# Expert blocks of 32 token slots on quarters of TensorE instead of 64 on halves

## The chip, the cores and the metric

The kernel runs on one core of a Trainium2 chip. The metric is the device time of one execution in microseconds. Its median before the change is 1385.75 us over three runs (1383.36 to 1388.35). All data are float32.

## The reference

A backbone of two layers over 512 latent tokens of width 1024 (with 256 context tokens for the attention of layer 0). Layer 0 mixes tokens by attention, layer 1 by a chunked gMLP; after each comes a mixture of 16 experts with hidden width 512, of which every token takes two. The change lies in the mixture. Cut to what matters:

```python
def moe_ffn(t, w_router, router_bias, w_gate, w_up, w_down):
    scores = jax.nn.sigmoid((t @ w_router).astype(jnp.float32))
    sel = scores + router_bias.astype(jnp.float32)
    ...                                  # best group of 4 experts, then the best 2 in it: eidx
    wts = jnp.take_along_axis(scores, eidx, 1)
    wts = wts / jnp.sum(wts, -1, keepdims=True)
    ...                                  # assignments sorted by expert, padded to blocks
    def expert_block(args):
        xblk, e = args
        hid = jax.nn.silu(xblk @ w_gate[e]) * (xblk @ w_up[e])
        return hid @ w_down[e]
    yb = lax.map(expert_block, (xb, block_e)).reshape(n_rows, d)
    y = jnp.zeros((n_tok + 1, d), jnp.float32).at[row_tok].add(yb.astype(jnp.float32) * row_w[:, None])
    return y[:n_tok].astype(t.dtype)
```

## The kernel before, in words

`backbone` writes one program for each engine; semaphores order them. SP issues all loads of weights, ACT (ScalarE) the stores, POOL (GpSimd) the gathers.

**Routing.** In `moe(l)` VectorE chooses two experts for each token, TensorE ranks the assignments by a product with a triangle, and VectorE computes how many blocks of BLK = 64 slots each expert needs (at least one), the table of the experts' first blocks, and each assignment's slot. Which token sits in a slot is found block by block: `onehot` compares the slots with 0 to 63 for both assignments (L956 to L958) and steps the slots back by 64 (L959), `index` on TensorE multiplies the one-hot with the token numbers (L1264), and VectorE casts the column to int32 as `gidx` (L962). Three such rounds come before the first block, and one lies in each block. 

**Gathers.** An indirect DMA (L437) fetches the 64 token rows of a block into `xga`. A GpSimd copy (L442) hands them to `xg`, and the next gather starts then: one is in flight.

**A block.** The loop runs over the blocks of an expert. TensorE waits for the turned rows `xT` and the expert's gate and up weights, then for each half h of the hidden width multiplies 64 slots by 256 columns of gate (L1301, PSUM partitions 0 to 63) and of up (L1303, partitions 64 to 127), side by side on two halves of its columns. After each half ScalarE takes silu of the gate part (L641), and VectorE multiplies by the up part (L995), while TensorE goes on with the other half. TensorE turns the hidden rows (L1311), ScalarE copies them out of PSUM (L643), and the down product (L1327) runs in two groups of eight records, 512 columns each, the index product between them. In the same block the next block's rows are turned (L1269) and VectorE applies scale and shift (L965, L967). VectorE multiplies the output by the gate row (L1005), and ScalarE issues two stores to `expert_rows` (L648). A matmul of float32 shows as two records.

The loops of ScalarE, VectorE and GpSimd take two blocks in each turn; where the number of blocks is odd, TensorE hands them an empty one at the end. ScalarE's loop begins with a small Silu (L636), before which its activation table is loaded.

**Weights.** Gate, up and down of an expert are 2 MB each. There are three sets of buffers. `follow` on SP waits until an expert's last block is through gate and up (for down: through the down product), and then issues the loads of the expert three further on into the same buffers (L302). At each change of expert TensorE reads that expert's first and last block from the table (L1284, L1285).

At the end of the mixture GpSimd waits for the stores and gathers for each token its two rows (L472), and VectorE adds them to the tokens.

## Time and profile before

| what | value |
|---|---|
| median of 3 runs | 1385.75 us |
| the profiled execution | 1385.64 us, span 1383.9 us |
| PE busy | 1173.4 us (85%) |
| PE weight loads busy | 662.0 us (48%) |
| DVE busy | 543.8 us (39%) |
| ACT busy | 245.3 us (18%) |
| POOL busy | 191.8 us (14%) |
| moved by DMA | 335.32 MB, mean 242 GB/s |
| granted TensorE clock, mean | 0.924 of full speed |

PE is TensorE's matmuls, PEld its weight loads, which overlap them, DVE is VectorE. The span runs from the first to the last instruction; the execution's own time is 1.7 us longer. Waits and the issue of DMAs are not counted as busy; rows with ACTq or SPq are such issues. The granted clock is told as a share of full speed: 1.00 is 2.4 GHz and 0.50 is 1.2 GHz.

### The profile page before, as it was taken

The page shows a single profiled execution, that of the slowest core. Times are in us where ns is not written, and L with a number is a line of the kernel's source. Part 1 is how long each engine was busy: PE and PEld are TensorE (multiplying, and loading weights), DVE is VectorE, ACT ScalarE, POOL GpSimd, SP SyncE. Part 2 cuts the span into 40 slices and gives each one's busy share as a digit, 9 for nine tenths or more (in the row PEclk, how much of TensorE's full clock was granted, in tenths as well). Part 3 has the DMA queues.
Part 4 walks back from the last instruction along what each step waited for, and adds up shares of the span by engine and source line. Part 5 has one row for each costly group of instructions (what it writes and reads, how often), then busy time and mean ns, then how long its engine had stood idle before and what let it go on. Part 6 is the DMA issues. An engine that isn't in the chain of part 4 may idle for free.

```text
span 1383.9 us, 18949 instructions
## 1 busy us (share of the span) xinstructions
PE 1173.4 (85%) x6946; PEld 662.0 (48%) x6947; DVE 543.8 (39%) x1319; ACT 245.3 (18%) x606; POOL 191.8 (14%) x166
## 2 busy tenths in 40 slices
PE   3999799998985999999983399999679999999940
PEld 0444344454453665665542244444445666655620
DVE  0246543462465333333323603045543333333338
ACT  0212333342020111111112111010201111111110
POOL 0012000000001111111111332200011111111123
PEclk9999999998985999999987699999679999999975
DMA  9921499980045999739995681121659996689933
GB/s 328 382 73 61 144 357 347 363 308 31 31 169 190 359 383 377 260 106 365 380 379 200 234 298 61 61 91 47 257 193 380 379 375 212 227 284 374 371 122 129
DMA packets 142758, 335.32 MB, mean 242 GB/s; under 512 B 6872, under 2 KB 9344, under 8 KB 142592
## 3 DMA queue, kind: packets, MB, share of 16 engines
q1 hardware_dynamic: 122400, 286.88, 57.0%
q10 hardware_dynamic: 13696, 25.38, 5.5%
q0 software_dynamic: 6624, 22.55, 5.4%
q8 instruction: 24, 0.39, 0.1%
q14 instruction: 14, 0.11, 0.0%
HBM read 315.40 MB, written 27.79 MB: 248 GB/s over the span
## 4 chain that ended last, share of the span: by engine, by line
PE 74%; DVE 9%; DMA 6%; SPq 6%; issue 2%; ACT 1%; POOL 0%; ACTq 0%; DVEq 0%; PEldq 0%; POOLq 0%
PE PS L1301 13%; PE PS L1327 11%; PE PS L1303 9%; PE PS L1234 8%; PE PS L1385 8%; PE PS L1144 7%; SPq L302 4%; PE PS L1164 3%; PE PS L1080 3%; PE PS L1264 2%; PE PS L1175 2%; DMA ring<-in_e_up_dram 2%; DMA RD<-expert_rows,yidx 2%; PE PS L1311 2%; PE PS L1269 2%
## 5 line engine op out<-in xcount | busy, mean ns | idle before, releaser
L1301 PE MATMUL PS<-ring,RE 128*64 128x256 f32 x1120 | 254.9, 387 | 22.4 <-DVE RE L967 10.3
L1303 PE MATMUL PS<-ring,RE 128*64 128x256 f32 x1120 | 255.3, 387 | 0.0
L1301 PEld LDWEIGHTS PS<-ring,RE 128*64 128x64 f32 x1120 | 154.6, 140 | 80.2 <-issue 45.3
L995 DVE TENSOR_TENSOR RE<-RE,PS 64x256 f32<-64x256 f32 x100 | 42.3, 423 | 350.0 <-ACT RE L641 350.0
L1303 PEld LDWEIGHTS PS<-ring,RE 128*64 128x64 f32 x1120 | 154.7, 140 | 28.6 <-issue 7.0
L1327 PE MATMUL PS<-ring,RE 128*64 128x512 f32 x560 | 136.2, 602 | 0.0
L1234 PE MATMUL PS<-ring,uT 128*128 128x512 f32 x256 | 111.2, 593 | 1.9 <-ACT G L605 1.1
L1385 PE MATMUL PS<-ring,uT 128*128 128x512 f32 x256 | 110.0, 592 | 0.0
L442 POOL COPY RFW<-RE 64x1024 f32<-64x1024 f32 x50 | 51.5, 1031 | 409.4 <-PE PS L1269 380.1
L1301 PE MATMUL PS<-uT,RE 128*64 128x256 f32 x416 | 95.0, 388 | 4.9 <-DMA RD<-in_e_up_dram 3.9
L1303 PE MATMUL PS<-RD,RE 128*64 128x256 f32 x416 | 95.3, 388 | 0.0
L1144 PE MATMUL PS<-ring,uT 128*128 128x512 f32 x192 | 84.4, 592 | 0.0
L1385 PEld LDWEIGHTS PS<-ring,uT 128*128 128x128 f32 x256 | 48.6, 190 | 60.7 <-issue 60.7
L1234 PEld LDWEIGHTS PS<-ring,uT 128*128 128x128 f32 x256 | 48.2, 190 | 60.7 <-issue 58.4
L437 POOL DMA_INDIRECT RE<-tokens,gidx x52 | 58.3, 1121 | 123.4 <-DVE gidx L962 121.9
L643 ACT ACTIVATE RE<-PS 128x128 f32<-128x128 f32 x100 | 27.7, 277 | 260.9 <-PE PS L1311 258.2
L641 ACT ACTIVATE RE<-PS 64x256 f32<-64x256 f32 x100 | 36.9, 369 | 202.0 <-PE PS L1303 193.1
L1301 PEld LDWEIGHTS PS<-uT,RE 128*64 128x64 f32 x416 | 57.5, 140 | 28.3 <-issue 15.5
L1080 PE MATMUL PS<-ring,silu_c 128*32 128x512 f32 x384 | 51.3, 655 | 23.2 <-DMA ring<-in_w_ada_dram 15.4
L1303 PEld LDWEIGHTS PS<-RD,RE 128*64 128x64 f32 x416 | 57.4, 140 | 6.6 <-issue 1.6
L437 POOL DMA_INDIRECT RFW<-tokens,gidx x2 | 2.3, 1166 | 398.0 <-DVE gidx L962 398.0
L1327 PEld LDWEIGHTS PS<-ring,RE 128*64 128x64 f32 x560 | 38.5, 136 | 39.4 <-issue 37.0
(214 smaller groups left out, 1482.3 us busy)
## 6 DMA issues: line engine op xcount, KB each, us to landing
ring<-in_w_ada_dram SPq DMA_DIRECT2D x24, 2048.0 KB, 11.7
ring<-in_e_gate_dram SPq DMA_DIRECT2D x22, 2048.0 KB, 16.6
ring<-in_e_up_dram SPq DMA_DIRECT2D x22, 2048.0 KB, 19.3
ring<-in_e_down_dram SPq DMA_DIRECT2D x22, 2048.0 KB, 19.9
uT<-in_e_gate_dram SPq DMA_DIRECT2D x10, 2048.0 KB, 17.0
RD<-in_e_up_dram SPq DMA_DIRECT2D x10, 2048.0 KB
RFW<-in_e_down_dram SPq DMA_DIRECT2D x10, 2048.0 KB, 21.9
ring<-in_b_win_dram SPq DMA_DIRECT2D x4, 2048.0 KB, 8.2
```

Source lines behind the costliest of these rows:

```text
L302: sp.dma_start(dst, src).then_inc(w_in[b], 16)
L437: nc.gpsimd.indirect_dma_start(out=rows, out_offset=None, in_=hscr[l], in_offset=bass.IndirectOffsetOnAxis(ap=gidx[0:BLK, par:par + 1], ax ...
L442: nc.gpsimd.tensor_copy(xg, xga).then_inc(xg_rd[l], 1)
L995: V_.tensor_tensor(hid[:, 256 * h:256 * h + 256], gs[:, 256 * h:256 * h + 256], PS[BLK:P, h, 0:256], ALU.mult).then_inc(hid_rd[l][h], 1)
L1080: ins = mm(PS[32 * g:32 * g + 32, bank, :], silu_c[:, k, :], w[:, k, :], start=(kk == 0), stop=(kk == 1))
L1144: ins = mm(PS[:, 4 + i % 3, :], a[:, k, j * P:(j + 1) * P], w[:, k, :], start=(k == 0), stop=(k == DC - 1))
L1164: ins = mm(PS[:, 6, :], V[:, k, kv * HD:(kv + 1) * HD], PT[:, k, :], start=(k == 0), stop=(k == NKT - 1))
L1234: ins = mm(PS[:, 2 * (j % 2) + half, :], uT[:, k, j * P:(j + 1) * P], w[half][:, k, :], start=(k == 0), stop=(k == DC - 1))
L1301: mm(PS[0:BLK, h, 0:256], xT[:, k, :], wg[:, k, 256 * h:256 * h + 256], start=(k == 0), stop=(k == DC - 1))
L1303: ins = mm(PS[BLK:P, h, 0:256], xT[:, k, :], wu[:, k, 256 * h:256 * h + 256], start=(k == 0), stop=(k == DC - 1))
L1327: ins = mm(PS[BLK * half:BLK * half + BLK, 5, :], hidT[:, k, :], wd[:, k, 512 * half:512 * half + 512], start=(k == 0), stop=(k == FC - 1))
L1385: ins = mm(PS[:, 4 + i % 4, :], uT[:, k, j * P:(j + 1) * P], w[:, k, :], start=(k == 0), stop=(k == DC - 1))
```

## The change

BLK becomes 32. The four parts of gate and up (gate and up, each in two halves of 256 columns) become four matmuls side by side on 32 columns each of TensorE, in one PSUM bank; one semaphore releases all of them. The gate parts lie on partitions 0 to 63 and the up parts on 64 to 127, so silu and product now take 64 partitions of 128 columns, twice. The hidden rows are turned in two turnings of 64 partitions, and the down product runs on four quarters of 256 columns each, so that a block leaves in four stores of 32 rows and 256 columns. The token numbers of all blocks (NCOL = 52 columns at most, with four spare) come from one accumulated product before the loop: a slot is cut into its low five bits and the rest, each is made one-hot, the second scaled by the token number. Gathers go to two buffers in turn, each by a column that GpSimd first copies to `gcol`; `xg` is now on RE. The number of blocks that the tables allow for grows from 32 to 48, and the compare with the thresholds from 7 to 15 for each expert.

```diff
-BLK = 64
+BLK = 32
+CG = P // BLK
...
                 pool.wait_ge(ix_rd[l], 1)
-                gather(0, xg, x0_in[l])
-                pool.wait_ge(ix_rd[l], 2)
-                gather(1)
+                gather(xg, x0_in[l], gidx[:, 0:1])
+                gather(xga[1], xg_in[l][1], gidx[:, 1:2])
+                gather(xga[0], xg_in[l][0], gidx[:, 2:3])
...
                         g = gg * 2 + par
-                        pool.wait_ge(xg_in[l], g * 16 + 16)
+                        pool.wait_ge(xg_in[l][1 - par], gg * 16 + 16)
+                        pool.nop(nofuse=True)
+                        nc.gpsimd.tensor_copy(gcol[:, 1 - par:2 - par], gidx[:, bass.ds(g + 3, 1)]).then_inc(gc_used[l], 1)
                         pool.wait_ge(xt_pe[l], g + 1)
                         pool.nop(nofuse=True)
-                        hand_over()
-                        pool.wait_ge(ix_rd[l], g + 3)
+                        nc.gpsimd.tensor_copy(xg, xga[1 - par]).then_inc(xg_rd[l], 1)
+                        pool.wait_ge(gc_used[l], g + 1)
...
-                        gather(par)
+                        gather(xga[1 - par], xg_in[l][1 - par], gcol[:, 1 - par:2 - par])
...
                 with act.Fori(0, pairs) as gg:
                     A(warm[:, :], ones[:, 0:1], ACT.Silu)
                     for par in range(2):
                         g = gg * 2 + par
+                        act.wait_ge(gu[l], g + 1)
                         for h in range(2):
-                            act.wait_ge(gu[l][h], g + 1)
-                            A(gs[:, 256 * h:256 * h + 256], PS[0:BLK, h, 0:256], ACT.Silu).then_inc(silu_rd[l][h], 1)
+                            A(gs[:, P * h:P * h + P], PS[0:2 * BLK, 0, P * h:P * h + P], ACT.Silu).then_inc(silu_rd[l][h], 1)
+                        for h in range(2):
                             act.wait_ge(ht_pe[l][h], g + 1)
-                            A(hidT[:, 2 * h:2 * h + 2, :], PS[:, 3 + h, 0:2 * BLK].rearrange("p (k s) -> p k s", k=2),
+                            A(hidT[:, h, :, :], PS[:, 3 + h, 0:2 * BLK].rearrange("p (h s) -> p h s", h=2),
                               ACT.Copy).then_inc(ht_rd[l][h], 1)
                         act.wait_ge(y_ev[l], g + 1)
                         act.nop(nofuse=True)
-                        for q in range(2):
-                            act.dma_start(yscr[l][bass.ds(g * BLK, BLK), 512 * q:512 * q + 512],
+                        for q in range(CG):
+                            act.dma_start(yscr[l][bass.ds(g * BLK, BLK), 256 * q:256 * q + 256],
                                           ysb[par][BLK * q:BLK * q + BLK, :]).then_inc(y_st[l][par], 16)
...
+                link(V_.tensor_copy(yidx[:, :, :], slot[:, :, :]))
+                link(V_.tensor_scalar(sli[:, :, :], yidx[:, :, :], BLK - 1, None, ALU.bitwise_and))
+                link(V_.tensor_copy(slo[:, :, :], sli[:, :, :]))
+                link(V_.tensor_tensor(shi[:, :, :], slot[:, :, :], slo[:, :, :], ALU.subtract))
+                V_.tensor_tensor(ohlo, slo[:, :, :].rearrange("p k t -> p (k t)").unsqueeze(2).broadcast_to([P, 2 * NT, BLK]),
+                                 iota_s.unsqueeze(1).broadcast_to([P, 2 * NT, BLK]), ALU.is_equal)
+                for k in range(2):
+                    for j in range(NT):
+                        ins = V_.tensor_scalar(ohhi[:, NT * k + j, :], iota_b, shi[:, k, j:j + 1], tokid[:, j:j + 1],
+                                               ALU.is_equal, ALU.mult)
+                ins.then_inc(oh_rd[l], 1)
+                dve.wait_ge(ix_pe[l], 1)
+                V_.tensor_copy(gidx[:, :], PS[0:BLK, 6, 0:NCOL]).then_inc(ix_rd[l], 1)
...
-                onehot(link)
-                for b in range(3):
-                    if b == 2:
-                        dve.wait_ge(x0_in[l], 16)
-                    dve.wait_ge(ix_pe[l], b + 1)
-                    index(b % 2)
-                    onehot(link)
                 affine(l, NT - 2)
...
                         dve.wait_ge(xt_pe[l], g + 2)
                         x_evac(lnk)
-                        dve.wait_ge(xg_in[l], g * 16 + 16)
-                        dve.wait_ge(ix_pe[l], g + 4)
-                        index(1 - par)
-                        onehot(lnk)
...
+                pe.wait_ge(oh_rd[l], 1)
+                for n in range(2 * NT):
+                    ins = mm(PS[0:BLK, 6, 0:NCOL], ohlo[:, n, :], ohhi[:, n, :], start=(n == 0), stop=(n == 2 * NT - 1))
+                ins.then_inc(ix_pe[l], 1)
...
-                        for h in range(2):
-                            for k in range(DC):
-                                mm(PS[0:BLK, h, 0:256], xT[:, k, :], wg[:, k, 256 * h:256 * h + 256],
-                                   start=(k == 0), stop=(k == DC - 1))
-                                ins = mm(PS[BLK:P, h, 0:256], xT[:, k, :], wu[:, k, 256 * h:256 * h + 256],
+                        for k in range(DC):
+                            for q in range(CG):
+                                w, h = (wg, wu)[q // 2], q % 2
+                                ins = mm(PS[BLK * q:BLK * q + BLK, 0, 0:256], xT[:, k, :], w[:, k, 256 * h:256 * h + 256],
                                          start=(k == 0), stop=(k == DC - 1))
-                            ins.then_inc(gu[l][h], 1)
...
-                        turn_hidden(0)
+                        ins.then_inc(gu[l], 1)
                         pe.wait_ge(xg_rd[l], g + 1)
                         pe.nop(nofuse=True)
                         turn_x()
+                        for h in range(2):
+                            pe.wait_ge(hid_rd[l][h], g + 1)
+                            pe.nop(nofuse=True)
+                            nc.tensor.transpose(PS[:, 3 + h, 0:2 * BLK], hid[:, P * h:P * h + P],
+                                                ident[0:2 * BLK, 0:2 * BLK]).then_inc(ht_pe[l][h], 1)
                         landed(2)
...
+                            for k in (h, h + 2):
+                                for q in range(CG):
+                                    ins = mm(PS[BLK * q:BLK * q + BLK, 5, 0:256], hidT[:, h, k // 2, :],
+                                             wd[:, k, 256 * q:256 * q + 256], start=(k == 0), stop=(k == FC - 1))
+                        ins.then_inc(dn_pe[l], 1)
```

## Rows read from the trace of the kernel before

**Rows 1.** Windows over the two expert loops: busy (records) by engine, granted clock, DMA share, GB/s.
```profile
437.50:741.10 303.60, 290.56 (x2300) 177.36 (x2300) 99.22 (x231) 43.01 (x114) 48.74 (x46) 0.97 0.87 308
1016.20:1329.50 313.30, 309.34 (x2500) 190.42 (x2500) 107.56 (x251) 46.66 (x124) 53.12 (x50) 0.99 0.85 302
```

**Rows 2.** Timeline of PE, layer 0, expert 7 and its end: start us, us, engine, what.
```profile
589.88 0.38 PE L1303 MATMUL PS<-ring,RE 128*64 128x256 f32 x1
...
596.60 0.38 PE L1301 MATMUL PS<-ring,RE 128*64 128x256 f32 x1
596.91 0.33 PE L1311 MATMUL PS<-ident,RE 64*128 64x64 f32 x2
597.08 0.67 PE L1269 MATMUL PS<-ident,RFW 64*128 64x64 f32 x8
597.70 1.94 PE L1327 MATMUL PS<-ring,RE 128*64 128x512 f32 x8
...
600.27 1.95 PE L1327 MATMUL PS<-ring,RE 128*64 128x512 f32 x8
602.04 0.38 PE L1303 MATMUL PS<-ring,RE 128*64 128x256 f32 x1
...
624.60 1.95 PE L1327 MATMUL PS<-ring,RE 128*64 128x512 f32 x8
626.65 0.40 PE L1301 MATMUL PS<-uT,RE 128*64 128x256 f32 x1
```

**Rows 3.** Window in the tail of layer 0's expert loop, columns as in rows 1.
```profile
640.00:730.00 90.00, 79.58 (x611) 47.53 (x609) 25.47 (x60) 12.93 (x32) 12.86 (x12) 0.94 1.04 379
```

**Rows 4.** Groups by line, whole span: busy us, mean ns of one, idle before and releaser.
```profile
L636 ACT ACT_TABLE_LOAD x25 | 32.1, 1283 | 119.4 <-issue 104.0 <-DVE table L941 15.4
```

**Rows 5.** Timeline of PE in the attention of layer 0.
```profile
161.04 1.92 PE L1080 MATMUL PS<-ring,silu_c 128*32 128x512 f32 x16
```

**Rows 6.** Timeline of ACT beside the block of rows 2.
```profile
591.13 1.14 ACTq L648 DMA_DIRECT2D expert_rows<-RFW  x2
592.58 1.28 ACT L636 ACT_TABLE_LOAD   x1 [4.52 <-issue]
...
593.98 0.36 ACT L641 ACTIVATE RE<-PS 64x256 f32<-64x256 f32 x1
597.28 0.28 ACT L643 ACTIVATE RE<-PS 128x128 f32<-128x128 f32 x1 [2.94 <-PE PS L1311]
```

**Rows 7.** Timeline of DVE beside the same block.
```profile
590.22 0.69 DVE L1005 TENSOR_TENSOR RFW<-PS,G 128x512 f32<-128x512 f32 x1 [0.53 <-PE PS L1327]
594.38 0.42 DVE L995 TENSOR_TENSOR RE<-RE,PS 64x256 f32<-64x256 f32 x1 [3.46 <-ACT RE L641]
```

**Rows 8.** Timeline at the start of layer 0's expert loop, POOL and PE.
```profile
433.69 1.18 POOL L442 COPY RFW<-RE 64x1024 f32<-64x1024 f32 x1 [6.61 <-DMA RE<-tokens,gidx]
...
437.54 0.68 PE L1301 MATMUL PS<-ring,RE 128*64 128x256 f32 x1 [5.09 <-DVE RE L967]
```

**Rows 9.** Timeline after the last matmul of layer 0's expert loop, DVE and POOL.
```profile
741.38 0.69 DVE L1005 TENSOR_TENSOR RE<-PS,G 128x512 f32<-128x512 f32 x1 [0.50 <-PE PS L1327]
...
748.34 0.69 DVE L1005 TENSOR_TENSOR RFW<-PS,G 128x512 f32<-128x512 f32 x1
...
753.05 0.95 POOL L472 DMA_INDIRECT RD<-expert_rows,yidx  x1 [11.44 <-DMA expert_rows<-RFW]
```

**Rows 10.** Windows around falls of the granted clock and where it held, columns as in rows 1.
```profile
317.30:320.80 3.50, 1.69 (x12) 1.08 (x11) 2.79 (x6) 1.37 (x3) 0.00 (x0) 0.99 0.00 0
...
689.90:692.80 2.90, 0.08 (x2) 0.00 (x0) 0.69 (x1) 0.32 (x1) 0.42 (x1) 1.00 1.06 400
692.80:696.20 3.40, 3.33 (x16) 2.18 (x18) 0.00 (x0) 1.17 (x2) 0.00 (x0) 0.50 1.02 331
...
709.90:716.70 6.80, 5.92 (x28) 3.75 (x30) 0.00 (x0) 0.00 (x0) 0.00 (x0) 0.50 1.03 360
726.00:728.90 2.90, 0.09 (x4) 0.06 (x2) 0.69 (x1) 0.34 (x1) 0.41 (x1) 1.00 1.05 398
```

More of the change, by code:

```diff
@@ L366, in follow @@
                     for j in range(3):
[L367 removed]
+                        sp.wait_ge(dn_pe[l] if j == 2 else gu[l], last)
                         sp.nop(nofuse=True)
@@ L405, in _ @@
             iota("thr", BLK, BLK, 0)
-            iota("pair", 2, 0, 0).then_inc(s_ic, 1)
+            iota("pair", 2, 0, 0)
+            iota("block", BLK, 0, 0).then_inc(s_ic, 1)
             pool.wait_ge(s_rope, 32)
```

128 lines of the change are left out of this document (45 added, 83 removed).

## The prediction, made before the change was run

> **What bounds the kernel now.** I first read the windows over the two expert loops. They last 303.6 and 313.3 us, 617 of 1383.9, and TensorE is busy for 96 and 99% of them at a granted clock of 0.97 and 0.99, while DMA moves 300 GB/s [rows 1]. TensorE's timeline says what a block is: one block starts at 589.88, the next at 602.04, so 12.16 us, or about 12.46 where the next block is another expert's. Inside are 32 steps of 0.217 us for gate and up (589.88 to 596.60, two column halves side by side), the turning, eight steps of 0.43 us for down in two groups and the index product [rows 2]. TensorE is the bound, but DMA is near: in the tail of the first layer it runs full, 379 GB/s [rows 3].
>
> **How many blocks.** ScalarE loads its table once for each pair of blocks, 25 times in all [rows 4], so 50 blocks, of which each layer's last may be padding. Counting the reference's routing for its inputs gives, over experts 0 to 15, blocks of 64 of 1 1 1 2 2 1 3 4 1 1 1 1 1 1 1 1 (23) and 1 1 1 1 1 3 2 4 2 2 1 1 1 2 1 1 (25), which agrees: 48 and two of padding. With 32 slots these become 2 1 2 3 4 2 5 8 2 2 1 2 1 2 1 1 (39) and 1 2 1 1 1 5 4 8 4 3 2 1 1 3 1 2 (40): 79 blocks, each to be under 617/79 = 7.8 us if the loops are to gain.
>
> **A block of 32, TensorE.** Do four quarters run side by side? The 16 matmuls of L1080, four quarters wide and 512 columns, take 1.92 us, which is four steps of 0.43 and a drain [rows 5]; the halves of now have the same step. So gate and up need 16 steps of 0.217: 3.47 us, and down eight of 0.217: 1.73 us. 5.2 us of matmul a block, 411 in all, against 48 x 10.4 = 499.
> But one counter now releases all of gate and up, so that silu, product, turning and copy stand open between them and down. From the block's start: the last step starts at 3.27 and ends 0.38 later, 3.65; ScalarE answers in 0.04 (596.91 + 0.33 to 597.28) [rows 2, 6]; silu of 128 columns 0.28 (the copy of 128 columns in [rows 6]), 3.97; VectorE answers in 0.04, and its product of 128 columns takes 0.29 (0.42 for 256 and 0.69 for 512 [rows 7]), 4.30; TensorE answers in 0.14 and turns in 0.28, 4.72; copy 0.04 + 0.28, TensorE 0.14: down starts at 5.18. The eight turnings of x (0.67 us [rows 2]) fit inside, the second half of the chain runs 0.2 behind the first and is hidden by down's first group. Down to next gate is 1.77 as now (600.27 to 602.04): **6.95 us**. Bounds: silu and product as dear as for 256 columns, +0.2; no turnaround between engines longer than counted, -0.1.
> The Trainium skill, TensorEngine Tiling (Array Packing), section PSUM Bottleneck, warns that packing quickens the matmuls and not the reading of PSUM; by matmul time alone the block would be 5.2, by the chain of rows just given it is 6.95, and the trace is on the page's side.
>
> **ScalarE's queue.** The change makes its two stores a block four, and keeps the Silu warm-up at the top of each pair of blocks. Now: product of y from 590.22 to 590.91, stores issued at 591.13, two in 1.14 us, table load at 592.58 for 1.28 us, silu at 593.98 [rows 6, 7]; this is 4.10 after the block's start and lies beside 6.9 us of matmuls. All 25 pairs load the table [rows 4]. After: product starts at 0.34 and takes 0.42 (0.76), stores at 0.98, four in 1.14 + 2 x 0.64 = 2.42 (3.40), 0.31 to the table load (3.71), 1.28 (4.99), silu at 5.11. It is wanted at 3.69. So each block that opens a pair is 1.42 us late: **8.37 us**. In the other block the stores end at 3.40, 0.3 before silu: hidden, but with nothing to spare. Behind the late silu wait product, turning and copy; x (two VectorE ops of 0.4, ready near 6.9) is late for nobody.
> 19 late blocks in each layer (the first pair loads its table before the loop): 38 x 8.37 + 41 x 6.95 = 603 us.
>
> **Change of expert.** TensorE's queue reads two table entries: from the last down group to the next gate 2.05 us (624.60 to 626.65) against 1.77 [rows 2]. That group is now 1.72 us of matmul, and will be 0.86. If the reading starts with it, the stall is 1.2; if it starts with the first group, 0.5; I take 0.75 and 0.5 more at each third expert. 30 changes: 22 + 5, of which 11 fall on late blocks, where TensorE waits anyway: +16. The Trainium skill, TensorE: Matmul & The Clock Gate, gives TensorE a queue of 64 with look-ahead (the table at its head); by it both groups would be queued at once and the stall be 0.5, some 4 us less. No row decides it.
>
> **Weights.** An expert is 6.29 MB; at 379 GB/s with its gathers and stores (0.26 MB a block) some 18.0 us. Loads run three experts ahead and start when the expert's buffers come free. I walk the experts: a third of a load 6.0 us, one after the other, the first 2.2 us after its release. With 64 slots and 12.17 the same walk gives 301.5 and 311.3, so it holds. With 32 slots expert 7 (8 blocks, 60 us) lets the loader idle, the one-block experts behind it then wait: 15 us in the two layers (12 to 25 for 5.8 to 6.3 us a third).
> First blocks run at half clock until some 6 us in, as now: +5.
> Loops: 603 + 16 + 15 + 5 = 639, against 617: **+22**.
>
> **Beside the loops.** Removed: per block three one-hot ops, a step back and a cast of VectorE, eight index matmuls; in the loop only the latter were on the path and are in the sum. Before the first block, one product waits on four small chained ops, one of 256 columns and eight of 36 (about 2.4 us), 16 matmuls for 8 (+0.9) and the wider threshold compare (+0.3): the first gather goes out about 2 us later, but the third one-hot and the 3.2 us of affine work ahead of the x product no longer follow its landing: gate comes from turned x in about 1.0, not 5.09 us [rows 8]. Net -2 a layer. GpSimd: copy of 1.2, some 0.7 to the gather, 1.2 to issue it and 6.6 until it has landed [rows 8]: 9.7 for one in flight, more than 7.7, but two are in flight: hidden with 5 us over, and its column copy too. With one in flight it would be +2 a block.
> At the end, the padding block goes in layer 1 (40 is even; 25 was not): the second y product came 7 us after the first, and the final gathers 12 us after the last matmul [rows 9]; four stores for two cost 1.3 back. -6 and -1. Together **-11**.
> Without anything else: 1385.6 + 22 - 11 = 1397 us. The sum is made against the profiled execution, 1385.6 us, 0.1 below the median.
>
> **The clock.** In a late block TensorE has only short turnings between 3.47 and 6.60: 3.1 us. In this trace it fell to half (1.2 of 2.4 GHz) at 692.8 after 2.9 us of nothing, again at 709.9, and at 320.8 after 3.5 us in which it was busy for 1.7, nearly all turnings; it held after 2.9 us at 726.0 [rows 10]. So such a gap is about where it falls. I take half of the 38 late blocks: 19. One fall costs half of the busy time in it: 1.7 (692.8) to 3.0 us (709.9), 2.3 x 19 = 44, less the 15 us of waiting for weights that late blocks make up: **+29**. 1426.
>
> **Cases.**
> Clock falls, 1427, own range 1410 to 1450: chance 0.48.
> Late silu, clock holds: 1397 (1388 to 1408): 0.27. For it: the turnings in the gap, and 726.0.
> The other side: silu is not late (table load or stores finish inside the 3.69 us). All 79 blocks at 6.95 = 549, changes 27, weights 32 (the loader then decides oftener), 5: 613, -4 and -11: 1371, faster by 1%. It turns at about 7.35 us for the mean block. Against it: the load of 1283 ns in all 25 pairs; for it: the sums rest on 0.3 us of slack, and loops from 5.8 us a third would give 8 back: 0.20.
> The quarters don't run together: 79 x 5.2 more, over 1750; [rows 5] speak against it: 0.02. Rest, slower still (stores delay silu in both blocks, more falls): 0.03.
>
> **Range.** 1388 to 1448: it leaves out the fast case and the worst. Faster by over 0.3% (4 us, about what can be told) 0.22, within it 0.07, slower 0.71.
>
> **What would show it.** 79 blocks, 40 table loads; first matmul of gate to first of down 5.2 in one block and 6.6 in the other, silu 1.4 us late in every second, with "issue" before the table load; steps of 0.217 with four quarters; granted clock in the loops near 0.93; TensorE's waits for weights of some 15 us behind expert 7; final gathers 6 us after layer 1's last matmul. I am wrong if mean blocks are at 7.0, if gates take more than 3.5, or if the clock stays at 1.00.

## The result and the profile after

The changed kernel takes 1391.2 us (median of 12 runs, 1384.8 to 1395.6) where the kernel before took 1385.8 (12 runs beside it). The ratio is 1.0041, 95% interval 1.0026 to 1.0056: slower, by 5 to 6 us and not by 41. A second set of ten runs gave 1389.5, ratio 1.0034 (1.0014 to 1.0053). The profiled execution took 1388.1 us, its span is 1386.2.

The two loops over the experts first, as windows (busy us and records of TensorE, its weight load, VectorE, ScalarE, GpSimd, then granted clock, DMA share, GB/s); they answer to [rows 1]:
```profile
432.00:744.60 312.60, 264.73 (x4134) 174.56 (x4134) 78.40 (x196) 60.35 (x194) 83.90 (x118) 0.96 0.82 294
1012.00:1337.80 325.80, 275.71 (x4240) 180.18 (x4240) 80.10 (x201) 61.17 (x198) 84.45 (x118) 0.94 0.79 283
```
They last 638.4 us for 616.9, so +21. TensorE, busy 96 to 99% of them before, is now busy for 85%. The rest of the kernel gave 19 us back.

TensorE's timeline, two blocks of one expert in layer 0, answers to [rows 2]:
```profile
597.98 3.66 PE L1292 MATMUL PS<-ring,RE 128*32 128x256 f32 x64
601.57 0.68 PE L1264 MATMUL PS<-ident,RE 32*128 32x32 f32 x8
603.29 0.45 PE L1301 MATMUL PS<-ident,RE 64*128 64x64 f32 x2 [1.03 <-DVE RE L995]
603.93 1.93 PE L1308 MATMUL PS<-ring,RE 128*32 128x256 f32 x32 [0.20 <-ACT RE L650]
605.66 3.66 PE L1292 MATMUL PS<-ring,RE 128*32 128x256 f32 x64
...
610.12 0.45 PE L1301 MATMUL PS<-ident,RE 64*128 64x64 f32 x2 [0.18 <-DVE RE L995]
610.77 1.93 PE L1308 MATMUL PS<-ring,RE 128*32 128x256 f32 x32 [0.20 <-ACT RE L650]
612.49 3.66 PE L1292 MATMUL PS<-ring,RE 128*32 128x256 f32 x64
```
Gate and up are 64 records (32 matmuls) in 3.66 us, so sixteen steps with four quarters in each. The first block takes 7.68 us (605.66 less 597.98), the second 6.83 (612.49 less 605.66). The difference stands in the gap ahead of L1301: TensorE waits 1.03 us for the hidden product in the first, 0.18 in the second. In the first, from the last matmul of gate (601.64) to down (603.93), it does nothing but turn for 2.3 us.

Why it is late is in ScalarE's timeline beside the same two blocks (answers to [rows 6]) and VectorE's (to [rows 7]):
```profile
598.96 1.89 ACTq L655 DMA_DIRECT2D expert_rows<-RE  x4
601.16 1.28 ACT L642 ACT_TABLE_LOAD   x1 [4.84 <-issue]
...
602.57 0.41 ACT L647 ACTIVATE RE<-PS 64x128 f32<-64x128 f32 x2
...
606.64 1.76 ACTq L655 DMA_DIRECT2D expert_rows<-RE  x4
609.38 0.43 ACT L647 ACTIVATE RE<-PS 64x128 f32<-64x128 f32 x2 [5.38 <-PE PS L1292]
```
```profile
598.32 0.42 DVE L1001 TENSOR_TENSOR RE<-PS,G 128x256 f32<-128x256 f32 x1 [1.44 <-PE PS L1308]
```
From the first block's start: stores at +0.98, four of them in 1.8 to 1.9 us, table load at +3.18, silu at +4.59. In the second block, which has no load, silu starts at +3.72 (609.38 less 605.66). By its wait for the hidden product, 25 of the 40 blocks that open a pair are late, by 0.75 us on the mean.

From the page, a group by line over the whole span (busy us, mean ns, idle before), which answers to [rows 4]:
```profile
L642 ACT ACT_TABLE_LOAD x40 | 51.3, 1283 | 201.6 <-issue 181.9
```
Forty table loads: 40 pairs, 79 blocks and one of padding.

What TensorE waited for, first layer's loop and then the second's (us in total, times, longest):
```profile
PE PS L1301 <- DVE RE L995: 16.8, 39, 1.1
PE PS L1292 <- DMA ring<-in_e_up_dram: 12.4, 2, 9.1
...
PE PS L1292 <- DMA RD<-in_e_up_dram: 2.3, 1, 2.3
PE PS L1308 <- DMA ring<-in_e_down_dram: 1.0, 1, 1.0
...
PE PS L1301 <- DVE RE L995: 17.2, 40, 1.0
PE PS L1292 <- DMA RD<-in_e_up_dram: 9.9, 1, 9.9
...
PE PS L1292 <- DMA ring<-in_e_up_dram: 5.3, 3, 3.9
PE PS L1308 <- DMA ring<-in_e_down_dram: 2.3, 2, 1.2
```
The lines with DMA are the weights: 15.7 and 17.5 us, 33 in all.

A fall of the clock, as windows (columns as above) and in TensorE's timeline; they answer to [rows 10]:
```profile
1175.00:1182.00 7.00, 5.99 (x104) 4.21 (x104) 1.45 (x5) 2.04 (x6) 2.29 (x4) 1.00 0.14 37
1183.30:1186.70 3.40, 3.40 (x39) 2.15 (x35) 0.42 (x1) 0.00 (x0) 0.88 (x2) 0.51 0.12 39
```
```profile
1176.89 3.66 PE L1292 MATMUL PS<-ring,RE 128*32 128x256 f32 x64
...
1182.17 0.45 PE L1301 MATMUL PS<-ident,RE 64*128 64x64 f32 x2 [1.01 <-DVE RE L995]
1182.82 3.27 PE L1308 MATMUL PS<-ring,RE 128*32 128x256 f32 x32 [0.20 <-ACT RE L650]
1185.79 4.10 PE L1292 MATMUL PS<-ring,RE 128*32 128x256 f32 x64
```
The down group takes 3.27 us for 1.93 and gate 4.10 for 3.66. The gap ahead of it is the one shown above, 2.3 us with turnings in it; there the clock held, here it fell to half. Twelve such falls lie in the loops. Eight come behind a gap like this inside a block (in one of them TensorE waited for down weights and not for the hidden product), four behind a wait for gate and up weights.

Start of layer 0's loop and the final gathers behind layer 1's (answers to [rows 8] and [rows 9]):
```profile
425.80 1.14 POOL L445 DMA_INDIRECT RE<-tokens,gidx  x1 [272.89 <-DVE gidx L967]
428.98 1.06 PE L1264 MATMUL PS<-ident,RE 32*128 32x32 f32 x8 [4.34 <-DMA RE<-tokens,gidx]
432.04 5.24 PE L1292 MATMUL PS<-ring,RE 128*32 128x256 f32 x60 [2.00 <-DVE RE L974]
...
1342.34 0.96 POOL L478 DMA_INDIRECT RD<-expert_rows,yidx  x1 [11.30 <-DMA expert_rows<-RE]
```
The first gate is at 432.0 and not at 437.5. The first gather has landed 3.2 us after its issue, where rows of 64 took more than twice that. The final gathers go out 4.5 us after layer 1's last matmul (its loop ends at 1337.8) and no longer 12.

**The loops, block by block.** From each block's first gate matmul to its first down matmul an undisturbed block takes 5.11 us, from there to the next gate 1.72. Taken over all 79 blocks of the trace:

| us | changed | single store | one read less |
|---|---|---|---|
| 79 blocks of 6.83 | 540 | 540 | 540 |
| over 5.11, gate to down (late silu, gate at half clock, first blocks) | 37 | 19 | 64 |
| over 1.72, down to next gate (change of expert, weights, down at half clock) | 61 | 82 | 56 |
| sum | 638 | 641 | 660 |

The last two columns belong to experiments below. Of the 37, late silus are 19, gate at half clock is 16 (4 of it in the two first blocks), and 3 are waits for down weights.

### The profile page after: what moved, and what is told of

The parts are those of the page before. It is cut to its first block, busy times and chain, and to the rows that moved or that the text cites. A ratio compares the mean times of both kernels' runs of the same rounds, so it can differ in the third digit from the quotient of the medians.

```text
span 1386.2 us, 27277 instructions
## 1 busy us (share of the span) xinstructions
PE 1105.8 (80%) x10504; PEld 642.0 (46%) x10505; DVE 482.9 (35%) x1205; ACT 275.4 (20%) x756; POOL 256.5 (19%) x309
## 4 chain that ended last, share of the span: by engine, by line
PE 57%; DVE 11%; DMA 9%; issue 8%; SPq 7%; ACTq 4%; ACT 4%; POOL 0%; DVEq 0%; POOLq 0%
PE PS L1292 10%; PE PS L1308 9%; PE PS L1230 8%; PE PS L1356 8%; PE PS L1140 7%; SPq L309 6%; ACTq L655 4%; DMA ring<-in_e_up_dram 4%; PE PS L1160 3%; PE PS L1076 3%; PE PS L1171 2%; DMA RD<-in_e_up_dram 2%; DMA RD<-expert_rows,yidx 2%; DVE mx L797 1%; DMA ring<-in_w_ada_dram 1%
## 5 line engine op out<-in xcount | busy, mean ns | idle before, releaser
L1292 PE MATMUL PS<-ring,RE 128*32 128x256 f32 x3712 | 223.9, 394 | 33.0 <-DMA ring<-in_e_up_dram 17.6
L1292 PEld LDWEIGHTS PS<-ring,RE 128*32 128x32 f32 x3712 | 143.1, 114 | 107.9 <-issue 53.2
L995 DVE TENSOR_TENSOR RE<-RE,PS 64x128 f32<-64x128 f32 x160 | 39.7, 288 | 343.1 <-ACT RE L647 343.1
L1308 PE MATMUL PS<-ring,RE 128*32 128x256 f32 x1856 | 121.2, 404 | 14.2 <-ACT RE L650 10.9
L647 ACT ACTIVATE RE<-PS 64x128 f32<-64x128 f32 x160 | 34.1, 262 | 310.6 <-PE PS L1292 306.0
L1292 PE MATMUL PS<-uT,RE 128*32 128x256 f32 x672 | 80.8, 394 | 16.3 <-DMA RD<-in_e_up_dram 12.2
L1308 PEld LDWEIGHTS PS<-ring,RE 128*32 128x32 f32 x1856 | 68.2, 114 | 44.5 <-issue 21.2
L1292 PE MATMUL PS<-RD,RE 128*32 128x256 f32 x672 | 80.4, 394 | 0.0
L462 POOL COPY RE<-RFW 32x1024 f32<-32x1024 f32 x40 | 41.3, 1032 | 203.4 <-PE PS L1264 203.4
L445 POOL DMA_INDIRECT RE<-tokens,gidx x4 | 4.0, 996 | 402.3 <-DVE gidx L967 401.7
L462 POOL COPY RE<-RE 32x1024 f32<-32x1024 f32 x40 | 41.3, 1031 | 197.9 <-PE PS L1264 197.9
L1292 PEld LDWEIGHTS PS<-uT,RE 128*32 128x32 f32 x672 | 49.0, 114 | 41.7 <-issue 24.1
L1264 PEld LDWEIGHTS PS<-ident,RE 32*128 32x128 f32 x648 | 46.7, 139 | 41.6 <-issue 32.5
L1301 PE MATMUL PS<-ident,RE 64*128 64x64 f32 x158 | 35.7, 244 | 34.0 <-DVE RE L995 34.0
```

What stands on the lines that cost most here:

```text
L462: nc.gpsimd.tensor_copy(xg, xga[1 - par]).then_inc(xg_rd[l], 1)
L1264: ins = nc.tensor.transpose(PS[:, 2, f * BLK:(f + 1) * BLK], xg[:, f * P:(f + 1) * P], ident[0:BLK, 0:BLK])
L1292: ins = mm(PS[BLK * q:BLK * q + BLK, 0, 0:256], xT[:, k, :], w[:, k, 256 * h:256 * h + 256], start=(k == 0), stop=(k == DC - 1))
L1308: ins = mm(PS[BLK * q:BLK * q + BLK, 5, 0:256], hidT[:, h, k // 2, :], wd[:, k, 256 * q:256 * q + 256], start=(k == 0), stop=(k == FC - 1))
```

## The experiments

Loop times below run from the first gate to the start of the last down matmul in layer 0: before 303.1 us, changed 312.1.

**Is the loop paced by late silus, or by the loader?** The four stores become one:
```diff
-for q in range(CG):
-    act.dma_start(yscr[l][bass.ds(g * BLK, BLK), 256 * q:256 * q + 256],
-                  ysb[par][BLK * q:BLK * q + BLK, :]).then_inc(y_st[l][par], 16)
+act.dma_start(yscr[l][bass.ds(g * BLK, BLK), :].rearrange("s (q c) -> q s c", q=CG),
+              ysb[par]).then_inc(y_st[l][par], 16)
```


> The changed kernel (1391.2 us), with one store of 128 partitions a block in place of four of 32; nothing else. Theory 1 (ScalarE's queue): in the block that opens a pair the four issues, 1.8 us, and the table load of 1.28 us make silu 0.9 us late and down 0.7 late. One issue should take about 0.5 us, so the table load begins 1.3 us earlier and silu is on time: all blocks 6.83 us inside an expert, 38 x 0.75 = 28 us less, of which waits for weights give back a third to a half: 1372 to 1378. Falls of the clock inside experts should go too. Theory 2 (the loader decides): blocks get as short, but the waits for weights grow by as much, from 33 us to some 55: 1386 to 1391. Theory 3: one store of 128 rows costs as much to issue as four of 32: no change, 1391.

Measured: 1391.99 us, ratio 1.0066 (1.0041 to 1.0090); loop 315.9 us. ScalarE's issue takes 0.55 us for 1.8, the late silus are gone, TensorE's wait for the hidden product fell from 16.8 to 7.3 us in layer 0's loop, and the weights took it all:
```profile
PE PS L1291 <- DMA ring<-in_e_up_dram: 26.7, 3, 11.2
```
By the table, 19 us less at one place and 21 more at the other. It was more than the loader taking what the blocks gave. In the tail, where DMA is full, this kernel moved less than the changed one (first row this kernel, second the changed one):
```profile
640.00:730.00 90.00, 64.00 (x954) 39.91 (x954) 18.59 (x46) 13.71 (x44) 19.15 (x28) 0.91 1.00 356
```
```profile
640.00:730.00 90.00, 70.46 (x1106) 45.60 (x1102) 21.83 (x55) 17.25 (x55) 23.28 (x33) 0.98 1.05 384
```

**Silu left out.** ScalarE copies where it took silu, in the loops, so no table load is needed; the four stores stay. (L647 and the warm-up become ACT.Copy.)


> The changed kernel with a copy in place of silu in the expert loop and in the small activation at its top; the silu of the hidden rows is left out. If the lateness of every second block is the table load, no table is loaded in the loop, and silu's place starts on time with all four stores kept: 6.83 us in all blocks, the same gain as with one store, 1372 to 1378. If it is the four issues that do it, the even blocks stay 0.7 late and the time stays at 1391. If a table is still loaded at the loop's top, nothing changes and the trace shows 40 loads.

Measured: 1366.86 us, ratio 0.9882 (0.9848 to 0.9916); loop 304.4. ScalarE's timeline has no load behind the stores, and no block is late:
```profile
593.18 1.85 ACTq L655 DMA_DIRECT2D expert_rows<-RE  x4
...
595.92 0.43 ACT L647 ACTIVATE RE<-PS 64x128 f32<-64x128 f32 x2 [0.36 <-PE PS L1292]
```
So the stores alone fit, and the load on top of them is what is late. Layer 1 routes otherwise here, so only layer 0's loop is compared: -7.7 us. This run mends the late silu too, and its loop got shorter, where that of the single store got 3.8 us longer: the single store has a cost of its own, and the lower rate above goes with it.

**Half the weights.** Experts 4 to 16 of a layer load the first half of each of their weights, the other half keeps what was there.
```diff
-                        load_expert(l, t * 3 + par if e is None else e, par, j)
+                        load_expert(l, t * 3 + par if e is None else e, par, j, True)
```


> The changed kernel, in which the loads of experts 3 to 15 bring only the first half of each of their three buffers; the other half keeps an older expert's weights, which are multiplied as before. So the loader takes half as long. Theory 1 (TensorE waits 33 us for weights, some clock falls follow such waits): those 33 us go, 1391 - 33 = 1358, down to 1350 with the falls behind the waits. Theory 2 (weight waits stand beside other waits and are repaid): less than 15 us gained, 1376 or more. What the blocks then take is their own: 79 blocks, 30 changes of expert and the late silu.

Measured: 1365.29 us, ratio 0.9865 (0.9829 to 0.9901); loop 299.8, so -12.3. TensorE's waits for weights, 15.7 us in this loop of the changed kernel, are gone. Layer 1 routes otherwise here as well.

**Both at once**, half the weights and a single store:


> The run with half loads and the one with a single store together: experts 4 to 16 load the first half of their weights only (the other half keeps older weights, so the values are not the reference's, and the second layer routes otherwise), and y goes out in one store of 128 partitions. It leaves neither a late silu nor a wait for weights, so it shows what the blocks alone cost. By the blocks' own time, 39 of 6.83 us, 14 changes of expert at 0.8 and the thirds' 0.6 more come to about 281 us, and with the first experts' loads, which stay whole, 286 to 290 us for the first loop, where half loads alone gave 299.8. If it stays above 296, something else than silu and weights paces the blocks.

Measured: one run of 1329.0 us; loop 284.0.
```profile
427.10:711.30 284.20, 257.11 (x4134) 171.81 (x4134) 81.85 (x196) 60.51 (x194) 83.44 (x119) 0.99 0.52 180
```
DMA's share is 0.52 and the clock holds. On layer 0's 312.1 us the single store alone gives +3.8, silu left out -7.7, half the weights -12.3, and half the weights with a single store -28.1. Silu left out and half the weights add up to 20, so some 8 us show only when both limits are away: while one is there, less comes of taking the other away. The rest of the distance would be the single store's own cost, which doesn't show when the queues are half empty; that is argued and not shown. The 284 are 39 x 6.83 = 266 us and, for most of the rest, the changes of expert; no late silu and no wait for weights is left.

**Does the gap let the clock fall, and what does a fall cost?** Two filling matmuls that nothing reads go behind the turning of x:
```diff
 turn_x()
+for _ in range(2):
+    mm(PS[:, 1, 0:P], ones[:, :], ident[:, :], start=True, stop=True)
```


> The changed kernel with two matmuls of 128 columns more on TensorE in each block, behind the turn of x, where it would else stand idle until the hidden product; they write a bank of PSUM that nothing reads. They take 0.1 us. Theory 1, the gap of 2.35 us in a late block is what lets the granted clock fall (12 falls in the loops, each such block some 1.3 us longer): with the gap cut, fewer than 6 falls, 5 to 12 us faster, 1380 to 1386. Theory 2, the clock falls for another reason (the waits for weights), or the blocks that it lengthens would have waited for weights anyway: within 3 us of the changed kernel.

Measured: 1392.63 us, ratio 1.0062 (1.0037 to 1.0086); loop 317.4.
```profile
606.46 0.71 PE L1299 MATMUL PS<-ident,ones 128*128 128x128 f32 x4
607.42 0.45 PE L1303 MATMUL PS<-ident,RE 64*128 64x64 f32 x2 [0.25 <-DVE RE L995]
```
Four falls are left in the loops, two at the end of layer 0's and two in layer 1's, each behind a wait for weights. The eight behind gaps inside blocks are gone, so the gap was their cause. The filling takes 0.71 us and not the 0.1 that I expected (each matmul is two records in the trace), so that each block that was not late went from 6.83 to 7.24. Fifty-four blocks of the changed kernel were not late, so the filling costs up to 22 us; the loops grew by 4.7 only (642.3 for 637.6, first gate to last down matmul). Read from the changed kernel's rows, the eight falls had lengthened their down groups and the gates behind them by 11 us, and waits for weights are 26 us here for 33; together that is about the difference.

A second run was to put the filling into late blocks alone:
```diff
+for _ in range(2 * (1 - par)):
+    mm(PS[:, 1, 0:P], ones[:, :], ident[:, :], start=True, stop=True)
```


> The changed kernel with the two filling matmuls (0.71 us on TensorE's row) in the first block of each pair alone, the one whose silu is late; the other block is untouched. In the run with fillers in both, no fall of the clock was left in the first loop before its end, late blocks stayed at 7.54 us and the others went from 6.83 to 7.24. Theory 1, a fall costs what its block is longer by (8.6 to 9.1 us for 7.54): the falls stay away, the others stay at 6.83, so 12 falls by 1.2 us, some 10 to 15 us less what the waits for weights take back (about half, as with the late silu): 1380 to 1386 us, ratio 0.996 to 1.000. Theory 2, the blocks that a fall lengthens would have waited for weights in any case: waits grow by as much as the falls gave, 1388 to 1393 us.

Measured: 1406.52 us, ratio 1.0151 (1.0126 to 1.0176). It doesn't answer its question, for two reasons. On TensorE par is the place of the expert in the ring and not the parity of the block, so the filling stood in the blocks of every third expert. And this run has the late y of the next paragraph.

**Does the reading at a change of expert cost what its gap shows?** The lower bound comes from the register with the upper bound of the expert before:
```diff
-                    lo = pe.value_load(table[l][0:1, col(0)], min_val=0, max_val=MAXB)
+                    if lo is None:
+                        lo = pe.value_load(table[l][0:1, col(0)], min_val=0, max_val=MAXB)
```


> The changed kernel with the same saving of one read of the table at each change of expert but the first of three. It tells whether the 0.8 us at a change is on the path that sets the end. If it is: blocks before a change go from 7.6 to about 7.1 us, 22 changes, 1391 becomes about 1380 (ratio to the kernel before 0.996). If the weights' waits (33 us in the changed kernel) take what the reads give, as they did when the late blocks were mended by the single store: 1388 to 1393, ratio 1.002 to 1.005.

Measured: 1406.07 us, ratio 1.0138 (1.0109 to 1.0167), slower, which neither theory allowed. Blocks on time ahead of a change did come down, from 7.6 to 6.95 us. But VectorE's product of y began later behind down: 603.72 less 601.13 is 2.59 us, where the changed kernel has 606.00 less 603.93, 2.07. The stores, the table load and silu followed:
```profile
603.72 0.42 DVE L1001 TENSOR_TENSOR RE<-PS,G 128x256 f32<-128x256 f32 x1 [1.98 <-PE PS L1309]
```
```profile
604.36 1.75 ACTq L655 DMA_DIRECT2D expert_rows<-RE  x4
606.43 1.28 ACT L642 ACT_TABLE_LOAD   x1 [5.24 <-issue]
```
```profile
602.85 3.66 PE L1293 MATMUL PS<-ring,RE 128*32 128x256 f32 x64
...
608.55 0.45 PE L1302 MATMUL PS<-ident,RE 64*128 64x64 f32 x2 [1.43 <-DVE RE L995]
609.20 3.37 PE L1309 MATMUL PS<-ring,RE 128*32 128x256 f32 x32 [0.20 <-ACT RE L650]
```
Down starts 6.35 us after gate (609.20 less 602.85), the gap is 2.7 us and not 2.3, and behind it down ran at half clock in 18 of the 40 blocks that open a pair, where the changed kernel has 8. So half a microsecond on VectorE went with 27 us more between gate and down. Repeated on another chip:

> The kernel of the run reads, unaltered. If the program makes VectorE late, its product of y again begins 2.5 to 2.7 us behind the first down matmul in most blocks and the ratio is 1.011 to 1.017. If the chip or the moment did, 2.06 us in nearly all, and then the ratio is what the saved read is worth: 0.992 to 1.004.

Measured: 1411.33 us, ratio 1.0178 (1.0145 to 1.0212), y late in the same way, though the edit changes nothing of VectorE and GpSimd. So it is not a chance of one execution or one chip. But it isn't shown to belong to the program either. The two chips of these runs also have the other four traces with a late y, and no kernel with blocks of 32 is on record there without it, nor one with it on another chip (see the last section). No one program was traced both ways. What the saved reading is worth, and how much of the loss in this run comes from its edit, therefore stays open.

**Two stores of 64 partitions:**
```diff
-for q in range(CG):
+for q in (0, 2):
-    act.dma_start(yscr[l][bass.ds(g * BLK, BLK), 256 * q:256 * q + 256],
-                  ysb[par][BLK * q:BLK * q + BLK, :]).then_inc(y_st[l][par], 16)
+    act.dma_start(yscr[l][bass.ds(g * BLK, BLK), 256 * q:256 * q + 512].rearrange("s (q c) -> q s c", q=2),
+                  ysb[par][BLK * q:BLK * q + 2 * BLK, :]).then_inc(y_st[l][par], 16)
```


> The changed kernel with two stores of 64 partitions in place of four of 32 (the same bytes, the same rows in memory). The run with one store of 128 partitions had no late block left (ACT issue 0.55 us for 1.89) and yet was slower: 1392.0 us, its transfers at 328 GB/s in the middle of the first loop where the changed kernel has 349. If the loss there was the load that a store of 128 partitions puts on the transfers of weights by its shape, two stores lie between: issue about 0.96 us, late blocks 0.3 us late or not at all, rate 340 to 350 GB/s, 1380 to 1388 us. If instead the loader simply can't feed faster blocks, whatever the shape: blocks on time, waits for weights grown by as much, 1388 to 1393 us with the rate at 330 to 350 GB/s.

Measured: 1481.91 us, ratio 1.0683 (1.0655 to 1.0711). It did not lie between four and one. The same late y, and a wait that none of the others has, those with the late y included: VectorE may overwrite a buffer of y only when the store of two blocks before has landed, and it waited for that.
```profile
DVE RE L1001 <- DMA expert_rows<-RE: 129.4, 32, 6.6
```


> The kernel of the run two_stores, unaltered. If the program does it: 1475 to 1490 us again, with VectorE waiting 2 to 6 us for the landing of the store of two blocks before. If the chip or the moment did: 1380 to 1395 us.

Measured on another chip: one run of 1478.8 us, with 119.8 us of that wait. In layer 0's loop of the first of the two runs TensorE's wait for the hidden product grew with it, to 38.7 us from 16.8, and the loop to 364.6 us. Why two stores of this shape land so much later than one or four was not found.

**Are two gathers in flight needed?** GpSimd waits for each landing before the next gather:
```diff
+                        pool.wait_ge(xg_in[l][1 - par], gg * 16 + 32)
+                        pool.nop(nofuse=True)
```


> The changed kernel, but GpSimd starts a gather only once the one before it has landed: one gather in flight in place of two, with both buffers kept. A gather takes 5.9 us from issue to landing and the hand-over copy 1.03, which with the issue's 0.9 comes to about 7.9 us in a row, more than the 6.83 us of a block. Theory 1, the second gather in flight is what lets blocks of 6.83 us run: TensorE comes to wait for the gathered rows in each block that is not late, blocks of 7.9 us or more, +20 to +60 us. Theory 2, the copy and the issue overlap enough of it, or the late blocks give it time: within 5 us of the changed kernel.

Measured: 1394.12 us, ratio 1.0065 (1.0041 to 1.0089), beside the changed kernel once more:

> The changed kernel itself, unaltered, once more, beside the runs of this call. In the runs with one read less at a change of expert and with two stores of 64 partitions VectorE began the product of y 0.5 to 0.7 us later after TensorE's last down product than in the changed kernel (2.52 to 2.71 us behind the first down matmul, where the changed kernel has 2.06), though VectorE's own instructions had not been changed in either. Theory 1, the delay belongs to these programs: this run shows 2.06 again, and 1388 to 1394 us, ratio 1.002 to 1.006. Theory 2, it comes and goes with the execution or the chip: this run may show 2.5 to 2.7, and then some 1400 to 1406 us, and the loss in those two runs would say nothing of the edit.

Measured: 1389.53 us, so two in flight are worth 4.6 us. TensorE waited for the hand-over seven times, six of them in layer 0's loop:
```profile
PE PS L1266 <- POOL RE L462: 6.5, 6, 1.7
```
The mean block of 8 us, late ones and waits counted, leaves room for most gathers.

**The other half of the change on blocks of 64.** The kernel before with the one index product, slots' columns by GpSimd, and one gather in flight:


> One part of the change alone, on the kernel before (1385.8 us): blocks stay 64 slots on two halves, all token numbers come from one product before the loop, gathers stay one in flight, by a column that GpSimd copies. Theory 1: eight index matmuls, 0.44 us, leave TensorE's path in each of 48 blocks: 21 us, and the three rounds before the first block go, 2 to 5 us a layer: 25 to 30 less, of which the tail of layer 0, where the loader decides, gives back some 8: 1359 to 1368, faster than both kernels. Theory 2: the index matmuls fill time in which TensorE would wait for the copy of the second turned half (0.28 us and two answers, about 0.4 us after the turning), so that only the start gains: 1376 to 1381.

Measured: 1383.79 us, ratio 0.9991 (0.9973 to 1.0009). The eight index matmuls, 0.47 us together, are gone from each block, and it still takes 12.15, because in their place TensorE waits for the copy of the second hidden half that they had covered:
```profile
PE PS L1315 <- ACT RE L648: 17.6, 48, 0.4
```
So that half is turned earlier, after two of the four products with the first:
```diff
+                        pe.wait_ge(ht_rd[l][0], g + 1)
+                        down(0, (0,))
 (turn the second half)
+                        down(0, (1,))
+                        pe.wait_ge(ht_rd[l][1], g + 1)
+                        down(1, (2, 3)).then_inc(dn_pe[l], 1)
```


> This is the run index64 (blocks of 64 slots as before the change, all slot indices from one product) with one thing more: the second hidden half is turned on TensorE after two of the four products with the first half, not after all four, so that ScalarE's copy of that half (0.37 to 0.40 us) is over before TensorE has run out of products. Theory 1, the copy is the last thing that ends in each block of index64 (TensorE waited for it 17.6 us over the two loops): the blocks go from 12.15 to about 11.75 us, 40 of them give back some 16 us, the waits for weights take up part of that; 1365 to 1375 us, ratio 0.985 to 0.993. Theory 2, something behind the copy (the hand-over of the gathered rows, the evictions of y) is due at the same moment: the blocks stay above 12.0 us and the time is within 0.3% of index64's 1383.8.

Measured: 1358.14 us, ratio 0.9783 (0.9757 to 0.9809). Both theories had the time too high: blocks came to 11.70 us, and the gap at a change of expert went with it (11.70 there too, 12.06 at each third, where before it was 12.47 and 13.0), since twelve records (six matmuls of 512 columns) now stand behind the last wait:
```profile
646.11 1.08 PE L1314 MATMUL PS<-ring,RE 128*64 128x512 f32 x4
647.12 0.34 PE L1299 MATMUL PS<-ident,RE 64*128 64x64 f32 x2
647.38 2.80 PE L1314 MATMUL PS<-ring,RE 128*64 128x512 f32 x12
```
The earlier turn alone, on the kernel before:

> The kernel before with one thing more: the second hidden half is turned after two of the four products with the first half. Its index product of eight matmuls (0.47 us) still stands ahead of the second half's products. Theory 1, there the copy of the second half is hidden by the index product, so the turn comes early for nothing: blocks of 12.15 us as before, within 0.3% of the kernel before. Theory 2, the hand-over copy or the copy of the hidden half was the last to end there too: blocks of 11.9 us or less, ratio under 0.995.

Measured: 1378.60 us, ratio 0.9944 (0.9916 to 0.9971), though blocks stayed at 12.2, as theory 1 had it. What went is the gap at a change of expert, 12.47 to 12.2; I had left that out. Removing the index matmuls gives nothing alone, the earlier turn 0.6%, both 2.2%.

With the saved read on top:

> turn64, and at each change of expert TensorE takes the lower bound of the expert's slots from the register that held the upper bound of the one before, so one read of the table less for two of three experts. Where reads set the gap at a change (+0.75 us at each in the changed kernel), some 22 changes give 0.5 us each: 8 to 11 us below turn64, about 1360 us. If the loader decides by then (half_loads: 33 us of waits worth 20 us over both loops), the gain is handed to the waits for weights: within 3 us of turn64.

Measured: 1360.84 us, ratio 0.9810 (0.9787 to 0.9833): nothing more, for the reading is hidden already.

## Why the prediction was right or wrong

The direction was right, and so were the parts of the mechanism: late silus, changes of expert, waits for weights and falls of the clock are all there. Their sizes were not: 41 us slower was forecast and 5 measured. The measured 1391 lies outside the likeliest case's own range of 1410 to 1450. It does lie within the whole range of 1388 to 1448, but by luck: that end of the range came from the case in which the clock holds, and the clock fell twelve times. What failed is the term of the late silus, 54 us forecast and 19 measured, and with it the term of the clock that was built on it, 29 us net forecast and 11 measured behind gaps inside blocks. By the prediction's steps:

- **A block of 32, TensorE.** Forecast 6.95, measured 6.83, down at 5.11 and not 5.18; steps of 0.217 with four quarters. Right; 9 us too much over 79 blocks. The Trainium skill, TensorEngine Tiling (Array Packing), section PSUM Bottleneck, says that tiling does not speed up the reading of PSUM; this trace agrees, for matmul time alone would make 5.2.
- **ScalarE's queue.** Right in kind, in 40 pairs, "issue" ahead of the load and all. Mis-sized: a late block takes 7.54 to 7.70, not 8.37. I had priced the four stores at 2.42 us from issues of 64 rows, 0.64 from start to start; those of 32 rows take 0.32 with 0.48 between starts, 1.8 in all. Lateness came out at 0.7 to 0.85 instead of 1.42. And 25 of the 40 opening blocks were late, not 38: of the fifteen others two open a loop and thirteen follow a change of expert, whose 0.8 us or more let ScalarE catch up. 54 us forecast, 25 x 0.75 = 19 measured. This is the step that failed first, and the clock's term was built on it.
- **Change of expert.** 0.75 forecast, 0.8 measured (7.6 for 6.83), and 1.4 at each third, so 28 us for 30 of them. I had taken 11 us off where a change falls ahead of a late block; that is what the thirteen blocks above show, but here it shortens the count of late blocks. Both terms together: 70 us forecast, 47 measured. The Trainium skill, TensorE: Matmul & The Clock Gate (the table at its head), gives TensorE a queue of 64. My estimate from it was 0.5 at each; the rows of this case decide for 0.8.
- **Weights.** 15 us forecast, 12 to 25 the range, 33 measured. My walk had blocks of 8 us on the mean between loads; with faster blocks the loader decides oftener, which I had written under the fast case (32) and not carried into the others. The half loads show the price: 12.3 us of layer 0 alone.
- **The clock.** 19 falls forecast behind 38 gaps of 3.1 us, seven found behind 25 of 2.3 and one where down waited for its weights; the eight cost 11 us in both loops together, where I had 29 net of 44. The four falls behind waits for gate and up weights had no term. The run with one read less agrees with the step: its gaps are 2.7 us, and 17 of its 32 late blocks have down at half clock. A gap of 3.1 us was never run. My reading of [rows 10] was loose as well: of the 1.7 us busy ahead of the fall at 320.8 some 0.5 were matmuls (L1176) and not turnings. The term hung wholly on the lateness of silu, and that was the number with the least behind it.
- **The loops.** Without the clock 639 forecast, 638 measured. This is no confirmation: late silu and changes together came out 23 and the blocks 9 too high, weights 18 too low, and 18 are left for the first blocks and the clock, where 5 stood for the first blocks. With the clock's 29 the forecast was 668, 30 too high (the whole sum is 1426, where the case says 1427); the other 8 of the 38 us between forecast and profiled execution lie beside the loops.
- **Beside the loops.** -11 forecast, -19 measured. 5.5 at the first start, because a gather of 32 rows lands in 3.2 us and I had kept the 6.6 of one of 64; 8 between the loops, where the final gathers follow sooner also in layer 0 (8.7 us after the last matmul, from 12), and 6 behind the last.
- **Two gathers in flight** hide the gather as said; but one would have cost 5 us and not +2 a block.
- **The rivals.** That silu is not late (1371) was wrong in the changed kernel, but two runs made that case. The single store took 1392, with the lower rate of its own; the run without silu, whose stores are those of the changed kernel, took 1367, and its loops 610 us where the case has 613, though its layer 1 has a block less. So the case's sum was close, and its condition was not met. That the clock holds (1397, with 0.27) came nearest in time, but its condition was not met either: 35 us too much for late silus covered the falls that it left out and 18 us of waits for weights that it had too low.

## What to carry to other kernels

Two limits that hide each other have to be taken away together, for each alone shows less than it is worth (here -7.7 and -12.3 against -28.1 us): a walk of loads against blocks has to be done again for each case of the block's time. A term that hangs on another, like the clock's falls on the gap, is to be priced at both ends of the other's uncertainty before it goes into the likeliest sum. An experiment that comes out slower than every theory allows has to be run beside the unaltered kernel on the same chip before its loss is put down to its edit. And before a matmul is taken off the path, look at what it covers: here a copy of the same length stood behind it, and turning it two products earlier was what made the removal pay, 29 us where each alone gave 2 and 7.

## What the runs showed of the hardware that I had not expected

- Issue of a store costs by its rows and shape: 0.32 us for 32 partitions, 0.49 (kernel before) and 0.53 (two stores) for 64, but 0.55 for one of 128 partitions.
- One store of 128 partitions for four of 32, the same bytes, lowered the rate in the full stretch from 384 to 356 GB/s; two of 64 let single stores land so late that VectorE waited 129 us for them in all. Neither was explained.
- In six of the runs (one read less and two stores, each twice, the misplaced filling, and half the weights with a single store) the end of the last down matmul reached VectorE 0.4 to 0.6 us later than in the others, wherever GpSimd's gather and column copy were running just then, and the product of y began some 0.3 to 0.4 us behind the end of that copy. The rows of GpSimd and VectorE are in the same order and phase as in the changed kernel, where the product starts at the end of the gather's issue, as the copy begins. First the changed kernel (GpSimd, then VectorE), then the one with one read less:
```profile
611.97 0.88 POOL L445 DMA_INDIRECT RFW<-tokens,gcol  x1 [0.87 <-POOL RE L462]
612.86 0.20 POOL L459 COPY gcol<-gidx 32x1 int32 x1
...
612.83 0.42 DVE L1001 TENSOR_TENSOR RE<-PS,G 128x256 f32<-128x256 f32 x1 [1.44 <-PE PS L1308]
```
```profile
602.32 0.88 POOL L445 DMA_INDIRECT RFW<-tokens,gcol  x1 [0.85 <-POOL RE L462]
603.20 0.20 POOL L459 COPY gcol<-gidx 32x1 int32 x1
```
  The last down matmul ends at 603.06 there by the profile's model, and y begins at 603.72. What decides it stays open, and the runs can't tell program from chip. All six come from two chips, and no kernel with blocks of 32 is on record there without it. Of the six traces that have a gather running at that moment and no late y, five come from two other chips; for the first trace of the changed kernel the chip is not known. Half the weights and the single store, each alone, did not have it on another chip, and the two together had it in every block on one of the two. The test that is missing is the changed kernel itself on one of these two chips.
- The clock's fall behind a gap is not decided by the gap alone: the same 2.3 us with the same turnings held at 601.6 and fell at 1180.5.
